# The residual of a three-block transformer kept with features on partitions, with a second pair of activation buffers

## The reference

```python
# first block
h = h + concat([dilated_attention, gated_recurrence]) @ w_out
h = h + cross_attention(rmsnorm(h, norm_cross_g), rmsnorm(mem, norm_mem_g)) # ... @ w_co
h = h + square(relu(rmsnorm(h, norm_mlp_g) @ w_mlp_in)) @ w_mlp_out   # inner width 4096
h = rmsnorm(h, norm_final_g)
# then two layers (l = 0, 1)
xn = rmsnorm(h, ln_mix_l);  z = xn @ w_in_l       # latent attention, Fourier, differential attention, recurrence, gates
h = h + 0.5 * merged_branches @ w_out_l           # the kernel's factor 0.5 comes from its tanh form of the sigmoid gates
xn = rmsnorm(h, ln_ffn_l)
h = h + (silu(xn @ w_gate_l) * (xn @ w_up_l)) @ w_down_l              # inner width 2816
out = h
```

## Time and profile before

| | |
|---|---|
| median of three executions | 1212.49 us |
| the profiled execution | 1213.07 us |
| its span, first to last instruction | 1211.1 us |
| TensorE busy | 1198.2 us (99%) |
| VectorE busy | 842.4 us (70%) |
| ScalarE busy | 689.9 us (57%) |
| GpSimd busy | 40.0 us (3%) |
| DMA engines busy (queue q1) | 49.8% |

### The profile page before, as it was taken

How to read it: one execution, slowest core, us unless ns; L and a number is a source line. 1 busy time by engine, 2 the same in 40 slices (tenths; PEclk the granted TensorE clock), 3 DMA queues, 4 the chain that set the end, 5 groups by cost and what they waited for, 6 DMA issues and landing times.

```text
span 1211.1 us, 23685 instructions
## 1 busy us (share of the span) xinstructions
PE 1198.2 (99%) x10044; PEld 1121.4 (93%) x10044; DVE 842.4 (70%) x1195; ACT 689.9 (57%) x1144; POOL 40.0 (3%) x88
## 2 busy tenths in 40 slices
PE   8999999999999999999999999999999999999998
PEld 8998989998899999899999998899999989999987
DVE  6997767654476878988656554658789877666544
ACT  5897655553366764792544543557665925544432
POOL 1200100000000000011000000000000100000000
PEclk9999999999999999999999999999999999999999
DMA  9643445565544435434565565535344426555552
GB/s 366 233 147 128 173 146 192 192 207 180 205 165 149 142 138 174 143 139 159 190 199 185 189 198 204 174 140 174 108 172 146 169 106 209 175 191 192 183 203 102
DMA packets 30617, 211.50 MB, mean 175 GB/s; under 512 B 3376, under 2 KB 3760, under 8 KB 5680
## 3 DMA queue, kind: packets, MB, share of 16 engines
q1 hardware_dynamic: 30224, 209.84, 49.8%
q10 hardware_dynamic: 288, 0.14, 0.0%
HBM read 208.92 MB, written 1.05 MB: 173 GB/s over the span
## 4 chain that ended last, share of the span: by engine, by line
PE 85%; ACT 6%; DVE 5%; issue 2%; DMA 1%; SPq 0%; DVEq 0%; ACTq 0%
PE bank L552 84%; ACT w_hi L1226 3%; DVE w_lo L1750 2%; ACT W L1542 2%; PE bank L671 1%; DMA ring<-weight_pieces 1%; PE bank L919 1%; DVE x_lo L1869 0%; DVE stat L2205 0%; ACT W L1226 0%; DVE W L2145 0%; DVE W L2278 0%; ACT W L1513 0%; ACT W L1508 0%; ACT W L1498 0%
## 5 line engine op out<-in xcount | busy, mean ns | idle before, releaser
L1750 DVE TENSOR_TENSOR w_lo<-ring,w_hi 128x2048 fp32r<-128x2048 f32 (+1 forms) x180 | 409.1, 2273 | 238.0 <-ACT w_hi L1226 237.3
L1226 ACT ACTIVATE w_hi<-ring 128x1024 fp32r<-128x1024 f32 (+1 forms) x368 | 366.5, 1047 | 232.7 <-PE bank L552 210.5
L552 PE MATMUL bank<-x_hi,w_hi 128*128 128x256 f32 x1840 | 260.5, 281 | 1.5 <-issue 1.4
L552 PE MATMUL bank<-x_hi,w_lo 128*128 128x256 f32 x1840 | 252.8, 277 | 3.1 <-DVE w_lo L1750 3.1
L552 PE MATMUL bank<-x_lo,w_hi 128*128 128x256 f32 x1840 | 247.5, 277 | 0.2 <-DVE x_lo L1869 0.2
L552 PEld LDWEIGHTS bank<-x_hi,w_hi 128*128 128x128 f32 x1840 | 230.5, 188 | 6.0 <-ACT x_hi L1226 1.9
L552 PEld LDWEIGHTS bank<-x_hi,w_lo 128*128 128x128 f32 x1840 | 229.0, 188 | 4.3 <-DVE w_lo L1750 4.1
L552 PEld LDWEIGHTS bank<-x_lo,w_hi 128*128 128x128 f32 x1840 | 226.8, 188 | 0.6 <-DVE x_lo L1869 0.6
L552 PE MATMUL bank<-W 128*32 128x32 f32 (+8 forms) x1552 | 75.6, 244 | 3.8 <-issue 2.2
L552 PE MATMUL bank<-w_hi,hid_hi 128*128 128x512 f32 x304 | 76.6, 389 | 0.0
L552 PE MATMUL bank<-w_lo,hid_hi 128*128 128x512 f32 x304 | 76.6, 389 | 0.0
(11 more groups left out here) (269 smaller groups left out, 1208.9 us busy)
## 6 DMA issues: line engine op xcount, KB each, us to landing
ring<-weight_pieces SPq DMA_DIRECT2D x191, 1024.0 KB, 4.9
W<-x_features SPq DMA_DIRECT2D x4, 256.0 KB, 4.9
ring<-weight_pieces SPq DMA_DIRECT2D x2, 512.0 KB, 5.7
h<-x SPq DMA_DIRECT2D x2, 512.0 KB, 6.7
W<-rg_weights SPq DMA_DIRECT2D x1, 1024.0 KB, 11.2
xs<-mem_features SPq DMA_DIRECT2D x1, 1024.0 KB, 12.8
oT<-mem SPq DMA_DIRECT2D x1, 1024.0 KB, 14.2
row<-rows SPq DMA_DIRECT2D x1, 1024.0 KB, 8.2
```

Source lines behind the costliest of these rows:

```text
L552: return nc.tensor.matmul(out, lhsT, rhs, start=first, stop=last)
L1226: return nc.scalar.activation(out, in_, ACT.Copy, scale=scale)
L1750: v.tensor_tensor(whole(w_lo, q), rows, whole(w_hi, q).bitcast(F32), ALU.subtract).then_inc(s_weight_low, 1)
```

## The change

`h` is kept with features on partitions (128 x 8 x 256). `wout`, `co`, `down` and `wd` become feat form; `down` and `wd` accumulate eight results of 256 tokens in all eight banks, where four of 512 stood. The transposes are gone: the norm steps write the high part from `h` itself, in four parts of two k, each once the results it needs are added (`norm_part`, `x_low`). For `cq`, `up` and `gu` these parts go to new buffers `y_hi` and `y_lo`, which lie over `xs` and `oT`; for `a` they go to x_hi and x_lo. Parts 0 to 2 behind `wout` are made while `wout` still runs.

The sum of squares now runs over partitions: ScalarE squares `h` element by element (`square`), VectorE adds the parts (`add_squares`), and TensorE adds over partitions with a product by a column of ones (step `columns`, or `layerstat`, which moved behind `a.1`). For the final norm VectorE also weights the squares with the squared gain. The first piece behind a norm has its two halves in two banks ("apart": each k gives hi and lo products for both halves, then the x_lo pass), so it takes one more bank. For `up` the factor is now applied to each piece: VectorE does max(u, 0) * factor^2 and then times u, from PSUM, and ScalarE's Relu is gone; the factor row comes between the halves of `up.1`. In `gu` VectorE has one more 128x512 operation per pair. `finalscale` is eight VectorE operations with a factor row from TensorE.

Small buffers were moved and paddings added: 7248 bytes more lie ahead of `h`, so `h`, `y_hi`, `y_lo` and the hidden rows start at a multiple of 8192 bytes from x_hi. The rope tables have a buffer of their own (GpSimd no longer waits for the mix before writing them), the row load is 512 KB instead of 1024 KB, and the output is stored by features and turned on the host.

```diff
-FEATURE = ("u", "y", "q", "k", "ck", "cq", "a", "f", "e", "up", "gu", "gate")
+FEATURE = ("u", "y", "q", "k", "ck", "cq", "a", "f", "e", "up", "gu", "gate", "wout", "co", "down", "wd")
...
-        h = sb("h", [P, TT, D])
+        sb("between_rows", [P, 20])
+        rope_rows = sb("rope_rows", [P, 2, S])
+        square_sum = sb("square_sum", [P, 2, S])
+        junk = sb("junk", [P, D], BF16)
+        rrow = sb("rrow", [P, S])
+        h = sb("h", [P, KT, S])
         xs = sb("xs", [P, TT, D])
         oT = sb("oT", [P, KT, S])
+        y_hi = nc.alloc_sbuf_tensor_at("y_hi", [P, KT, S], F32R, offset=nc.sbuf_base - 4 * 2 * KT * S)
+        y_lo = nc.alloc_sbuf_tensor_at("y_lo", [P, KT, S], F32R, offset=nc.sbuf_base - 4 * KT * S)
...
-        steps += [*ups[:4], ("params",), *ups[4:]]
+        steps += [pe(ups[0]), act(ups[0]), ("columns", "norm_mlp_g"), ("low", ups[2][-1]), dve(ups[0]), *ups[1:4], ("params",), *ups[4:]]
...
-            steps += [a[0], ("high", f0[-1]), ("low", f0[-1]), ("layerstat", l), a[1], f0, ("finalscale", l)]
+            steps += [a[0], ("high", f0[-1]), ("low", f0[-1]), a[1], ("layerstat", l), f0, ("finalscale", l)]
...
+            gus = proj("gu", l, range(22))
+            steps += [gus[0], ("columns", f"ln_ffn_{l}"), *gus[1:]]
...
-                rs = col("rs." + before, TT)
                 bank = fill(f"{before}.rstd", "m")
-                for tt in range(TT):
-                    ins = mm(bank[:, tt * P:(tt + 1) * P], rs[:, tt:tt + 1].broadcast_to([P, P]), ident, True, True)
+                for n, name in enumerate(("ln_mix_0", "final") if before == "ln_mix_0" else (before,)):
+                    rs = col("rs." + name, TT)
+                    for tt in range(TT):
+                        ins = mm(bank[:, n * S + tt * P:n * S + (tt + 1) * P], rs[:, tt:tt + 1].broadcast_to([P, P]), ident, True, True)
...
-                elif kind == "norm" and step[1] not in LOADED:
-                    name = step[1]
-                    for j in range(KT // 2):
-                        for _, tt, c0, n, s_in, value in norm_input("final" if name == "ln_mix_0" else name):
-                            if c0 < 256 * (j + 1) and c0 + n > 256 * j:
-                                pe.wait_ge(s_in, value)
-                        turns(f"{name}.{j}", lambda k, tt: h[:, tt, (2 * j + k) * P:(2 * j + k + 1) * P], 2)
+                elif kind in ("columns", "layerstat"):
+                    name = step[1] if kind == "columns" else ("final", "ln_mix_1")[step[1]]
+                    pe.wait_ge(s_ones, 1)
+                    pe.wait_ge(s_stat_sum, feature_stats.index(name) + 1)
+                    bank = fill(f"{name}.sum", "m")
+                    for n, src in enumerate((square_sum[:, 0, :], rrow) if name == "final" else (square_sum[:, 0, :],)):
+                        for tt in range(TT):
+                            ins = mm(bank[:, TT * n + tt:TT * n + tt + 1], src[:, tt * P:(tt + 1) * P], ones_col, True, True)
+                    full(ins, f"{name}.sum")
...
+                    elif name in ("q", "k", "u", "y", "a", "e", "f"):
+                        gemm(job, "g", p, "feat", parts=parts, between=between, apart=before is not None)
+                    elif name == "cq":
+                        gemm(job, "g", p, "feat", parts=parts, x_hi=y_hi, x_lo=y_lo, between=between, apart=j == 0)
...
-                    elif name in ("v", "wout", "b", "c", "hg"):
-                        gemm(job, "g", p, "tok", parts=parts, ks=ks, apart=(name, j) == ("wout", 0) and l is not None)
+                    elif name in ("v", "b", "c", "hg"):
+                        gemm(job, "g", p, "tok")
+                    elif name == "wout":
+                        gemm(job, "g", p, "feat", parts=parts, ks=ks, apart=j == 0 and l is not None)
                     elif name in ("up", "gu"):
-                        gemm(job, "m", p, "feat", parts=parts, between=between)
+                        gemm(job, "m", p, "feat", parts=parts, x_hi=y_hi, x_lo=y_lo, between=between, apart=j == 0)
...
+                        passes = ((w_hi, hid_hi), (w_hi, hid_lo), (w_lo, hid_hi))
+                        if j == 0:
+                            acc = []
+
+                        def accumulate(m, i):
                             w, x = passes[i]
                             for k in range(2):
-                                ins = mm(acc[tt, c][:, :], x[:, 2 * j + k, tt * P:(tt + 1) * P], w[:, k, 512 * c:512 * c + 512],
+                                ins = mm(acc[m][:, 0:S], half_of(w, q, k)[:, m * P:(m + 1) * P], x[:, 2 * j + k, :],
                                          i == j == k == 0, i == 2 and k == 1 and j == count - 1)
                             return ins
 
-                        if j < count - 1:
+                        if 0 < j < count - 1:
                             for i in range(3):
                                 if i == 2:
                                     wait_low(pe, q)
-                                for tt in range(TT):
-                                    for c in range(2):
-                                        ins = accumulate(tt, c, i)
+                                for m in range(KT):
+                                    ins = accumulate(m, i)
+                        else:
+                            wait_low(pe, q)
+                            for m in range(KT):
+                                if j == 0:
+                                    acc.append(fill(f"{tag}{m}", "g" if m < 3 else "m"))
+                                for i in range(3):
+                                    ins = accumulate(m, i)
+                                if j:
+                                    full(ins, f"{tag}{m}")
...
+            def norm_part(name, i):
+
+                x = x_hi if name[:6] == "ln_mix" else y_hi
+                gi = V_GAIN + GAINS.index(name) * KT
+                gain = col("gain.final", KT) if name == "ln_mix_0" else vec[:, gi:gi + KT]
+                for job in producers(name, i):
+                    wait_drained(act, job)
+                for k in (2 * i, 2 * i + 1):
+                    ins = copy(x[:, k, :], h[:, k, :], gain[:, k:k + 1])
+                ins.then_inc(s_norm_all, 1)
+
+            def square(name, i):
+
+                n = feature_stats.index(stat_of(name))
+                if i == 0 and n:
+                    wait_filled(act, f"{feature_stats[n - 1]}.sum")
+                elif i == 3:
+                    act.wait_ge(s_square_added, 3 * n + 1)
+                nc.scalar.activation(square_place(i), h[:, 2 * i:2 * i + 2, :], ACT.Square).then_inc(s_square, 1)
...
+                    for i in {"norm_cross_g": (3,), "norm_mlp_g": (2, 3), "ln_ffn_0": (3,), "ln_ffn_1": (3,)}.get(name, range(4)):
+                        norm_part(name, i)
+                        if i < 3:
+                            square(name, i)
+                    if name[:6] == "ln_mix":
+                        split_ahead(piece_after[name])
+                        square(name, 3)
+                    else:
+                        square(name, 3)
+                        split_ahead(piece_after[name])
...
+            def x_low(name, i):
+
+                hi, lo = (x_hi, x_lo) if name[:6] == "ln_mix" else (y_hi, y_lo)
+                gi = V_GAIN + GAINS.index(name) * KT
+                gain = col("gain.final", KT) if name == "ln_mix_0" else vec[:, gi:gi + KT]
+                dve.wait_ge(s_norm_all, 4 * (norms.index(name) - len(LOADED)) + i + 1)
+                for k in (2 * i, 2 * i + 1):
+                    ins = v.scalar_tensor_tensor(lo[:, k, :], h[:, k, :], gain[:, k:k + 1], hi[:, k, :].bitcast(F32), ALU.mult, ALU.subtract)
+                ins.then_inc(s_norm_low_all, 1)
+
+            def add_squares(name, i):
+
+                stat = stat_of(name)
+                n = feature_stats.index(stat)
+                dve.wait_ge(s_square, 4 * n + i + 1)
+                src = square_place(i)
+                if stat == "final":
+                    weight = col("gain.square", KT)
+                    for k in (2 * i, 2 * i + 1):
+                        if k == 0:
+                            link(v.tensor_scalar(rrow[:], src[:, k % 2, :], weight[:, k:k + 1], None, ALU.mult))
+                        else:
+                            link(v.scalar_tensor_tensor(rrow[:], src[:, k % 2, :], weight[:, k:k + 1], rrow[:], ALU.mult, ALU.add))
+                if i:
+                    v.tensor_tensor(square_sum[:], square_sum[:], src, ALU.add).then_inc(s_square_added, 1)
+                    dve.wait_ge(s_square_added, 3 * n + i)
+                if i == 3:
+                    v.tensor_tensor(square_sum[:, 0, :], square_sum[:, 0, :], square_sum[:, 1, :], ALU.add).then_inc(s_stat_sum, 1)
...
+                        if name == "norm_mlp_g" or name[:6] == "ln_mix":
+                            x_low(name, 2)
+                        x_low(name, 3)
```

(54 more changed lines are left out.)

357 lines of the change are left out of this document (153 added, 204 removed).

## The result

The changed kernel takes 1235.55 us (median of four, 1235.15 to 1236.31) against 1211.51 of the kernel before (four executions): a ratio of 1.0197, 95% interval [1.018, 1.0215], so 24 us slower where I forecast 3.3 us faster. The profiled execution took 1235.15 us.

What follows compares the result with a forecast made beforehand. TensorE was taken as the bound, busy 1198.2 of 1211.1 us. Removed work -18.2, added work +2.7 and waits +12.25 gave -3.3 us: 1209.8 for the profiled execution, 1209.2 by the median, range 1200 to 1216.5.

Steps and rivals of the forecast that it cites:

- I take nothing: In `down` and `wd`, 912 products of 512 columns becoming 1824 of 256 cost nothing, given the good rate.
- (a): At six norms, the 16 transposes of the residual on TensorE go: 10.6 us saved.
- (b): Behind the norms, the first products no longer wait for x_hi piece by piece, nor x_lo products run slow: 5.6 us saved.
- `down` and `wd` run at the poor rate: Rival: their 1824 products each take 0.0045 us more, +8.2 us, net +4.9, 1217.4 us; chance 0.13.
- (c): The two layers' `wout` become products with activations moving, 0.113 us each for 0.1175: 1.7 us saved.
- (e): Added on TensorE: 14 one-column sum products and 4 spreading the factor, 2.0 us, plus 0.7 for seven insertions: +2.7 us.
- The last rival: Each product costs a little beyond its columns, 1.2 ns over 1824: 2.2 us, net -1.1, 1211.4 us; chance 0.08.
- `co` to `up`: Added waits at this norm: 0.75 before the sums, 1.7 for the factor, 0.6 at `up.2`, in all +3.15 us.
- `gu.2`: Waits for its bank until the factor row is multiplied in, 1.05 us late, twice: +2.1 us.
- `down` to `a`: Layer 0 added waits: 1.25 for parts 2 and 3, 2.5 for weighted squares, 0.5 for `f.0` weights: +4.25 us.
- Behind `wd`: Layer 1 added waits: 1.25 for parts 2 and 3, 1.5 for w_hi and w_lo of `f.0`: +2.75 us.
- rival of larger waits: Each boundary loses as much as it gained: 1.4 times the 12.25, +4.9, net +1.6 us, 1214; chance 0.14.

Runs made afterwards that it cites:

- the exact place: Changed kernel with between_rows 16 floats instead of 20, so y_hi lies exactly 11 x 8192 bytes above x_hi: 1212.21 us, ratio 1.0008 to the kernel before.
- the run of the banks: Kernel with between_rows 16 floats, with column sums and factor rows of up and gu moved to three free banks: 1210.73 us, ratio 0.9991.
- the last kernel: Kernel with between_rows 16 floats, with layer 0's final-norm weighted squares moved from VectorE to ScalarE and two-column TensorE products: 1210.62 us, ratio 0.9983.
- e_best: Kernel with between_rows 16 floats, plus weighted squares on TensorE, up and gu sums and factor rows in free banks, later w_lo wait: 1208.43 us, ratio 0.9972.

## Why the prediction was wrong

**The step that failed** is "I take nothing, because the new operands stand to each other as those of the earlier trace rows do", with its count that hid_hi lies at x_hi's remainder after the change, and the same taken for granted of y in (a) and (b). It was arithmetic on sizes without the allocator's rounding. Both sets missed the place by 32 bytes. The rival "`down` and `wd` run at the poor rate" had the right mechanism and size (8.2 us, measured 7.8 alone), but I let it stop at hid; the larger part, 16 us, is y in `cq`, `up` and `gu`, for which I had no rival. Undoing the 32 bytes gives back 23.3 of the 24 us. Why TensorE is slower at the other places no run shows.

**The rest of the sum** can be read at the exact place. Stretches of TensorE's timeline between one first or last product and the next, in us, profiled executions of before (span 1211.1) and of the exact place (1209.0):

| stretch | before | exact | difference | predicted |
|---|---|---|---|---|
| to `co` | 157.39 | 154.91 | -2.5 | -2.2 |
| `co`, `up` | 101.04 | 101.68 | +0.6 | +1.1 |
| `down` | 86.84 | 86.93 | +0.1 | 0 |
| behind `down`, to the lora stage | 23.65 | 26.87 | +3.2 | +2.1 |
| layer 0 to the last merge | 200.38 | 202.32 | +1.9 | 0 |
| `wout0`, `gu` | 145.65 | 144.85 | -0.8 | -2.0 |
| `wd` | 59.63 | 59.82 | +0.2 | 0 |
| behind `wd` | 23.54 | 22.21 | -1.3 | +0.2 |
| layer 1 to the last merge | 204.12 | 201.68 | -2.4 | 0 |
| `wout1`, `gu` | 145.60 | 144.69 | -0.9 | -2.0 |
| `wd1` and tail | 63.26 | 63.05 | -0.2 | -0.3 |

The sum is -2.1 in these two executions and +0.7 between the medians (interval -0.1 to +2.2). Single executions move these stretches: the first one takes 154.2 to 155.7 us in the eight profiled executions of the changed form at a good place that have it unchanged. Point by point:
- (a), (b), (c) and the tail are borne out within that spread: `cq`'s stretch gives 2.5 of 2.2, and no h is turned. In (c) the first 35 to 60 products of each `wout` still start every 0.118 us, so 192 of them take 114.1 to 114.7 ns on average and not 113.
- (e) was put too low by half. A one-column product, and one that spreads the factor, shows as two in the trace, and the two take 0.22 us: the eight records of the four sums ahead of `f.0` take 0.88. So 18 products cost 4.0 us and not 2.0. The whole count bears it out: 912 + 48 more products of the residual, 96 transposes fewer and 2 x 18 make the 900 more that the page has.
- The last rival, a cost beyond the columns, is nothing: 226.7 ns for 512 columns is twice 113.3 within 0.1.
- `co` to `up`: 0.7, 1.36 and 0.17 us of wait, forecast 0.75, 1.7 and 0.6. `gu.2`: 1.14 each, forecast 1.05.
- `down` to `a`: parts 2 and 3 cost 0.7 us with the restarts, forecast 1.25, and `f.0` does not wait for its weights, forecast 0.5. `f.0` starts at T+15.0, forecast T+15.1, since the excess of (e) makes up for most of that; the wait for the weighted squares is 2.4, forecast 2.5. What I lacked is the clock. In the exact kernel TensorE's granted clock falls behind this wait (windows: length, busy of each engine, clock):

```profile
343.00:355.00 12.00, 11.87 (x100) 11.48 (x100) 10.74 (x22) 6.77 (x14) 0.00 (x0) 1.00 0.50 170
355.00:358.60 3.60, 1.38 (x13) 1.21 (x12) 3.46 (x6) 3.60 (x9) 0.00 (x0) 1.00 0.06 23
358.60:362.80 4.20, 4.20 (x25) 4.20 (x25) 3.76 (x18) 0.63 (x3) 0.00 (x0) 0.60 0.41 138
```

- 16 products went at 0.213 us for 0.113, near the 1.2 GHz level, 1.6 us. In the kernel with everything 128 bytes further on the same wait had no such thing behind it, and that stretch took 25.2, +1.6. Its rows:

```profile
357.04 0.58 PE L551 MATMUL bank<-stat,square_sum 128*128 128x1 f32 x4 [2.39 <-issue]
...
358.00:362.00 4.00, 4.00 (x36) 4.00 (x36) 3.56 (x18) 0.54 (x3) 0.00 (x0) 1.00 0.46 131
```

- `gu` to `wd`: 0.67 us of wait in each layer, unforeseen. The first piece of `down` and `wd` goes bank by bank, so its fifth product wants w_lo, and the kernel had it wait ahead of the first; I had cost the reordering by its product count alone. With 0.2 more for (e), 0.1 for `gu.2` and 0.2 for (c) this is the 1.2 us between -0.8 and -2.0.
- Behind `wd` I was 1.5 us too high: of the 1.5 for w_hi and w_lo of `f.0` about 0.5 came, and of the 1.25 for parts 2 and 3 about 0.7.
- Layer 0's levels have a new gap, among 192 tiny products. The first row is from before, the second from the exact place:

```profile
540.75 1.35 PE L552 MATMUL bank<-W 128*32 128x32 f32 x128 [0.16 <-issue]
```

```profile
542.29 1.29 PE L551 MATMUL bank<-W 128*32 128x32 f32 x121 [0.24 <-ACT W L1661]
545.22 0.27 PE L551 MATMUL bank<-W 128*32 128x32 f32 x7 [1.64 <-issue]
```

It stands behind the same product, the 4875th that the trace has of TensorE's (the 4874th in one), in each of the eleven kernels of the changed form, 1.6 to 2.7 us from start to start, also in the four that have 24 more records of products ahead of it. The two of the old form have none in this layer, and one of 1.9 to 2.2 in layer 1's levels, behind the 8264th. There the changed form has one too, of 1.2 to 2.0 behind the 8909th in nine of the eleven. TensorE waits for nothing that the profile shows. So the gap goes by the count of instructions, not by the step. That 900 more products shift a point at which TensorE's instructions run short is my reading; no run tested it.

Layer 1's -2.4 is mostly no gain of the change. In the profiled execution of before the granted clock falls behind the gap of 2.2 us, and half of 3.4 us, about 1.7, is lost; in the exact kernel's the gap is 1.7 us and the clock stays. Where it falls at this point in a changed kernel, as in the one 128 bytes on, the stretch takes 203.3 us and not 201.7. Before:

```profile
972.98 0.38 PE L552 MATMUL bank<-W 128*32 128x32 f32 x20 [2.01 <-issue]
```

```profile
970.70:973.70 3.00, 0.99 (x52) 0.81 (x38) 0.61 (x2) 1.53 (x3) 0.00 (x0) 1.00 0.00 0
973.70:977.10 3.40, 3.40 (x10) 2.69 (x9) 2.20 (x6) 0.00 (x0) 0.00 (x0) 0.50 0.02 5
```

My rival of larger waits (+1.6) lies nearer than the forecast to the +0.7 between the medians and further from the -2.1 of the two traces. Its nearness is luck: the waits that it named came to 8.8 us and not to more than 12.25, and (e), the w_lo wait and the clock, which it didn't name, made up for a part of that. The chances for slower, 0.10 by the poor rate and 0.17 in all, were too low: the change gave half the products new operand places.

## What to carry to other kernels

Treat the address of a moving operand against that of its weights as part of a product's price: print the addresses that the allocator gave, and compare them by the remainder, before taking a rate from another stage's rows. Where a change moves tensors, an experiment that moves them back by a few bytes, alone, is the cheapest first one. A wait taken from TensorE shows the next one behind it: count what the busiest helper engine has in its queue, and expect a part of the wait back (0.42 of 1.14 us in the run of the banks).

## What the runs showed that I had not expected

Products of 256 columns went at 113.3 ns where the moving operand's address lay 64 bytes past a multiple of 128 from the weights', and at 117.4 to 120.0 at each other multiple of 32 that I tried, with or without traffic from VectorE and ScalarE. With the weights moving, one place has two steady rates, 113.5 and 117.8, and the start of a stream chooses.

The clock can fall with no wait at all, and not in each execution. In the last kernel TensorE is busy throughout with the two-column products, and goes on at 0.54 of its clock for 17 products; in the profiled execution of `e_best`, the same code at this place, it didn't. A fall costs 1.6 to 1.7 us, as much as most edits here, so a part of the spread between executions is this: of the exact kernel's ten, the three longest (1213.6 to 1214.4 us) have a mean granted clock of 0.995 to 0.997, and the three shortest (1210.9 to 1211.5) have 0.999. The rows of the last kernel:

```profile
354.00:357.80 3.80, 3.80 (x37) 3.80 (x35) 0.62 (x1) 1.86 (x6) 0.00 (x0) 1.00 0.71 220
357.80:361.50 3.70, 3.70 (x20) 3.70 (x20) 3.02 (x18) 0.00 (x0) 0.00 (x0) 0.54 0.26 106
```
